# New words for the order of pieces in the two mixers, the two cross attentions and the two blocks

## The reference

```python
for layer in range(2):                       # first_block
    x = x + 0.5 * swiglu(rms_norm(x, ...), w_gate, w_up, w_down)
    h = rms_norm(x, mix_norm[layer])
    x = x + (diff_stickbreak_mixer if layer == 0 else mla_mixer)(h, ...)
    x = x + memory_cross_attention(rms_norm(x, ...), rms_norm(mem, ...), ...)
    x = x + 0.5 * swiglu(rms_norm(x, ...), ...)
for l in range(2):                           # second_block
    h = x @ w_cols
    mix = concat(gla(h_gla), rwkv7(h_rwkv), nsa(h_nsa)) @ w_out[l]
    x = layer_norm(ALPHA * x + mix, ...)
    x = layer_norm(ALPHA * x + swiglu(x, ...), ...)
```

## Time and profile before

| | us |
|---|---|
| median of 3 runs | 2518.86 (2516.48 to 2523.28) |
| the profiled execution | 2525.97 |
| its span, first to last instruction | 2524.2 |
| mean granted TensorE clock | 0.887 |
| PE, DVE, ACT, POOL busy | 2163.8, 1607.8, 1127.3, 433.6 |
| m0, from 208.1 to 426.0 | 217.9 |
| c0, from 426.0 to 497.0 | 71.0 |
| m1, from 876.0 to 1082.0 | 206.0 |
| c1, from 1082.0 to 1145.5 | 63.5 |
| b0, from 1336.3 to 1717.5 | 381.2 |
| b1, from 1919.9 to 2317.0 | 397.1 |

### The profile page before, as it was taken

The page is one execution under the profiler, slowest core; times in us unless marked ns, Lnnn a source line. Parts: engine busy times, 40 slices in busy tenths (PEclk is TensorE's granted clock), DMA queues, the critical chain, the costliest instruction groups (busy, mean ns, idle before and its releaser), DMA issues.

```text
span 2524.2 us, 33226 instructions
## 1 busy us (share of the span) xinstructions
PE 2163.8 (86%) x12512; PEld 1870.8 (74%) x12512; DVE 1607.8 (64%) x2915; ACT 1127.3 (45%) x2001; POOL 433.6 (17%) x393
## 2 busy tenths in 40 slices
PE   6999867699999977779999767879998766978997
PEld 6888756588888866767889555777887654767886
DVE  6867654487687667557765763646765674455765
ACT  4645562365465444335544412326544521234553
POOL 2410011122122100013200210001221120000223
PEclk9999887799999988789999876878998887678998
DMA  6555322155555532125554212014553212102552
GB/s 240 186 183 166 117 67 74 60 180 182 190 184 177 184 117 79 48 73 186 189 179 140 86 43 95 1 60 163 185 174 107 103 57 69 43 1 92 190 178 91
DMA packets 88720, 311.59 MB, mean 123 GB/s; under 512 B 9840, under 2 KB 12144, under 8 KB 88048
## 3 DMA queue, kind: packets, MB, share of 16 engines
q1 hardware_dynamic: 88272, 305.55, 37.1%
q10 hardware_dynamic: 288, 3.92, 0.4%
HBM read 308.38 MB, written 1.05 MB: 123 GB/s over the span
## 4 chain that ended last, share of the span: by engine, by line
PE 77%; DVE 14%; ACT 5%; issue 3%; POOL 1%; DMA 1%; DVEq 0%; SPq 0%; ACTq 0%; POOLq 0%
PE ps L124 74%; DVE scratch L139 5%; PE ps L129 3%; DVE w_lo L139 2%; ACT w_hi L134 2%; ACT scratch L134 1%; DVE stats L156 1%; DVE scratch L166 1%; DVE stats L151 1%; DVE scratch L145 1%; ACT scratch L165 1%; DVE stats L139 1%; DMA ring<-in_w 1%; ACT h L134 0%; POOL rows L139 0%
## 5 line engine op out<-in xcount | busy, mean ns | idle before, releaser
L139 DVE TENSOR_TENSOR w_lo<-ring,w_hi 128x1024 fp32r<-128x1024 f32 (+2 forms) x571 | 692.1, 1226 | 440.2 <-ACT w_hi L134 429.3
L124 PE MATMUL ps<-h,w_hi 128*128 128x512 f32 (+1 forms) x2720 | 877.4, 380 | 46.0 <-DVE h L151 19.1
L134 ACT ACTIVATE w_hi<-ring 128x1024 fp32r<-128x1024 f32 (+2 forms) x571 | 582.2, 1033 | 507.2 <-PE ps L124 500.2
L124 PE MATMUL ps<-h,w_lo 128*128 128x256 f32 x2416 | 687.1, 284 | 0.0
L124 PEld LDWEIGHTS ps<-h,w_hi 128*128 128x128 f32 x2720 | 503.6, 194 | 150.3 <-issue 32.1
L124 PEld LDWEIGHTS ps<-h,w_lo 128*128 128x128 f32 x2416 | 466.5, 193 | 0.0
L124 PE MATMUL ps<-f,w_hi 128*128 128x512 f32 (+1 forms) x1444 | 425.3, 360 | 6.0 <-DVE f L139 6.0
L124 PE MATMUL ps<-scratch 64*128 64x128 f32 (+10 forms) x2016 | 331.5, 358 | 72.7 <-DVE scratch L139 27.8
L124 PEld LDWEIGHTS ps<-scratch 64*128 64x128 f32 (+4 forms) x2016 | 280.6, 236 | 119.7 <-issue 51.2
L124 PE MATMUL ps<-f,w_lo 128*128 128x256 f32 x1184 | 334.9, 283 | 0.0
L124 PEld LDWEIGHTS ps<-f,w_hi 128*128 128x128 f32 x1444 | 259.4, 193 | 49.6 <-DVE w_lo L139 5.1
(11 more groups left out here) (122 smaller groups left out, 2152.7 us busy)
## 6 DMA issues: line engine op xcount, KB each, us to landing
ring<-in_w SPq DMA_DIRECT2D x520, 512.0 KB, 3.6
ring<-in_w SPq DMA_DIRECT2D x48, 384.0 KB, 3.8
ring<-in_w SPq DMA_DIRECT2D x16, 396.0 KB, 4.3
stage_consts<-in_cthree ACTq DMA_DIRECT2D x1, 1916.0 KB, 8.5
stage_consts<-in_ctwo ACTq DMA_DIRECT2D x1, 1915.0 KB, 7.5
stage_consts<-in_cone SPq DMA_DIRECT2D x1, 1339.0 KB, 6.5
ring<-in_w SPq DMA_DIRECT2D x9, 128.0 KB, 3.8
x<-in_x SPq DMA_DIRECT2D x4, 256.0 KB, 4.6
```

The lines of the kernel that those rows point to most:

```text
L124: return self.e.matmul(out, lhsT, rhs, start=start, stop=stop, skip_group_check=free)
L134: return self.e.activation(out, x, func, **k)
L139: return self.e.tensor_tensor(out, a, b, op)
```

## The change

Six words of the table WEAVE are replaced by others with the same letters, each as often as before. No function changes. What moves, told by pieces:

- m0: rs0 stands before lqa0; nk and both halves of qb come before lva; lva and ck0 come behind the first stick's first step; ck1 and ck2 stand together behind the third stick's first step; the first steps of sticks 7 and 6 come before sub0 and ck5, which stand together; the last steps of both come behind the first two turns of the output.
- m1: rs0 first; ck1 and ck2 before uq0; ck3 and ck4 behind hk; ck5 between kT5 and kT6; ck6 and ck7 late among the attention steps, whose lanes go in a regular round.
- c0, c1: another order of the lanes.
- b0: rp0 to rp4 without gp0 between them; rw2 before ga; rkk, rbon and rdec further ahead and np0 behind rdec; the delta rule from ri6 on before more of nc1 and of the attention.
- b1: ga before gp1; np0 before rkk; ri3 and ri4 before nk; ru, rG, rP and rS before or among nc1 and nS; the second round, from rm1,0 on, 13 places further ahead, with more attention steps behind its start.

```diff
--- before.py
+++ after.py
@@ -38,14 +38,14 @@
 
 
 WEAVE = {
-    "b0": ("rrgrrrrhgghhhghhhhhhrrrrhlhrrhhlrhhlrhhrrhrrhrhrrnrrnnnnnrnnrnwrnrnrnunnurwnrnuvurrwuruvuwrvrwru"
-           "ruvurrrrurvvrvrrwvrwrvrvrwrwvrwrvurwrwuwrrwuwrrrrvrrururvuvummmmmmmmmmmmmmmmmmmmmmmmmmmmmmmmmmmm"),
-    "b1": ("rrrrrrgrghghhhghhhrhhrhrhlhrrhhlhrrhlhrhrhrrrhrhnrrrnnrnnnnnrnrnrrnrnrunwvnurrnrvnruwurwrvuruwrv"
-           "urrvrrvruwrwrwvururvwrvrvwrvurwvruwrwurrrurrurwurvruwrwruvrvmmmmmmmmmmmmmmmmmmmmmmmmmmmmmmmmmmmm"),
-    "c0": ("ppppppcbdcbacbadadooooooooooooo"),
-    "c1": ("ppppppabdabcdabcdcooooooooooooo"),
-    "m0": ("qpqpqkykqbkvvkakbqbacsbbsaatbataasslsctacacssycaccyyactytcscattsscctostttstyyyooooooooooooooooo"),
-    "m1": ("yqpqqkqqkqqkqkqkkkhyttttttttuuuubcuayucuauyabacbbyababcabybacaabbcacbyaaybcabaccaacbccacbcoooooo"
+    "b0": ("rrrrrrgrhrgghrhhrhhhghhhrrhhhlrhhlhrhlhrrhrrhrrhnrrnnrrnnnnnrnrvnrwurwrnurnrnnrrnrnvrrurwvruwrru"
+           "rvrruwrrvuvrvrwruwvrururvwruwrvrurrrurvwruvrwuurwrvrwrwvvuwmmummmmmmmmmmmmmmmmmmmmmmmmmmmmmmmmmm"),
+    "b1": ("rrrrrrghggrhrhhlhrrhhghhhrhhrhhlhhrhlhrrhrrrrhrhnrrnrrnrrnnnnnrnrnrrnrrrnrurwnrvrnurrrrrnvrrnuru"
+           "vrwvruwrwrvuuvwrvuwrvurvwrurrrwrwrvruwrvuuwrvvruwwrvuurwvummwummmmmmmmmmmmmmmmmmmmmmmmmmmmmmmmmm"),
+    "c0": ("ppppppbadbacdbacdcooooooooooooo"),
+    "c1": ("ppppppbdabdcabdcacooooooooooooo"),
+    "m0": ("pqqqkkkpqbbkalbbaqsvyvstbkabactssyyacsaccastsctyaatccasttyctaccsttcacsoytsyyootsooooooooooooooo"),
+    "m1": ("pyqqqkkqyqyqqkqkqkkkhyyttttttyttuuuauuucuuabcaabccbabcaabccabbcaabccabbcyaabccabbcaayoaobcaboooo"
            "ooooooooooo"),
 }
 
```

## The result

The changed kernel takes 2443.8 us in the median of four runs (2442.4 to 2449.6), the kernel before beside it 2521.1: a ratio of 0.970, with a 95% interval of 0.968 to 0.972. Forecast were 2484 us and a range of 2450 to 2512. The sign was right and the size was not: 77 us went where 35 were forecast. The profiled execution has a span of 2440.4 us in place of 2524.2, 83.8 less.

The account below looks back on a forecast made before the run. TensorE and VectorE were taken to wait for each other in one fixed order, neither full; -7.5 (m0), -8.9 (m1), -1.8 (c0), -4.9 (b0) and -12.0 (b1) sum to -35.1 us, from 2518.9 to 2484, range 2450 to 2512.

Parts of the forecast that it names:

- the stop before rs0 with its cost: m0's start: TensorE idles 4.5 us before rs0 and a slow half projection adds 2.7, sum +7.2 us.
- The walks of VectorE in m0 and b1's front: VectorE's queue walked in new order with old durations: m0 -7.5, -6.7, -0.5 us; b1's front -6.5.
- b1's rm1,0: In b1, the second round's first product was to come about 26 us earlier.
- The work is the same piece by piece: All six stages: no matmul, split or transfer added or removed, so moves were costed with the trace's old times.
- a loss of 2.7 forecast: m0's start: half projection after the stop takes 8.30 us at clock 0.67 instead of 5.60, 2.7 more.
- -16.0: m1, first kT to output projection: 17.8 us of TensorE work gone, ck5's stop adds 1.8; between -20 and -12.
- +14.4: b1's last stretch: 20.3 us of work enters, 5.9 covered by idle time; ends +4.7 and +20.3.
- the slower rival: Blocks' mean clock falls from 0.78 to 0.737, cancelling the gain; at 0.72 the time is 2534 us; chance 0.07.
- a third of the idle time closes: m0, m1, b0, b1: 90 of 270 us idle may go, giving 2429 us; centre 2445, chance 0.12.
- No change: Seven or eight new look-ahead split stops in the two blocks eat 35 us; time 2518, chance 0.11.
- The clock rival: Blocks: waits among thinly spread small matmuls lower TensorE's granted clock, so the kernel gets slower; chance 0.07.
- theory B: From the experiments: TensorE's clock follows how much it stands still, so closing stops also speeds the matmuls around them.

Follow-up runs that it names:

- starts: Changed kernel with rs0 put back behind the first half projection in m0 and m1: 2442.1 us, ratio 0.968.
- m1_memory: Kernel before, with everything in m1 but the attention steps at its new places, the output's first two pieces still behind the attention: 2516.2 us, ratio 0.998.
- b1_held: Changed kernel with nS1, nS2 and eleven attention steps of b1 put back ahead of the second round: 2464.0 us, ratio 0.977.
- b1_dense: Kernel before, with every matmul of the attention steps of units 7 to 15 in b1 issued twice: 2533.7 us, ratio 1.004.
- m1_lanes: Kernel before, with only the 48 attention steps of m1 in the new regular round: 2523.7 us, ratio 1.001.
- m1_ck5: Changed kernel with the norm ck5 of m1 put back among the attention steps: 2450.4 us, ratio 0.973.

## Why the prediction was wrong in size and right in sign

The terms, in us, forecast and measured:

| place | forecast | measured |
|---|---|---|
| m0: start; to S0; to S5; to out; out | +7.2, -7.5, -6.7, -0.5, 0 | +7.0, -6.7, -9.7, -0.9, -1.9 |
| c0, c1 | -1.8, 0 | -5.0, +0.2 |
| m1: start; uq0; to kT0; to out; out | +0.7, +6.4, 0, -16.0, 0 | +1.3, +3.7, -1.0, -25.6, -3.1 |
| b0: front; to nc0; to rm1,0; to out; out | 0, -1.0, -6.6, +2.7, 0 | -0.7, -3.9, -5.2, +1.1, -2.8 |
| b1: front; to nc0; to rm1,0; to out; out | -6.5, +3.2, -23.1, +14.4, 0 | -5.8, +4.4, -27.4, +3.6, +2.3 |
| feed-forward stages | 0 | -7.7 |
| sum | -35.1 | -83.8 |

(The profiled execution of before lies 5 us above its median, that of after 1.5 us below, which is why the medians differ by 77 and the spans by 84.)

**What held.** The sign of every term that was not forecast at 0, and the stop before rs0 with its cost: 4.50 us and a slow lqa0 behind it, 7.0 in sum for 7.2, shown by putting rs0 back. That the price of the slow half projection fitted is in part luck: it was read behind m1's stop of 3.74 us, and behind that same stop the starts kernel lost nothing. The walks of VectorE in m0 and b1's front are within 1 us, except m0's middle, which was 3.0 us too small. uq0 came later, b1's rm1,0 came 28.8 us earlier (26 forecast), and its last stretch became longer. The sign rests on these.

**The step that failed: TensorE's clock was held fixed.** "The work is the same piece by piece", and so I moved pieces at the durations that they had. In this kernel a piece has no duration of its own. Of the 48.7 us between the two sums, 30.0 are matmuls that ran faster in the six stages (27.3 measured, against a loss of 2.7 forecast), 12.0 are idle time that closed beyond the forecast, and 6.7 lie in the feed-forward stages (by the stages' windows; the table ends f0 with TensorE's last instruction, 1 us earlier). The same steps of m1's attention took 50.0 us of TensorE (67.6 less 17.6) and then 41.6, at clocks of 0.80 and 0.94. Of the 9.6 us by which "-16.0" was too small, 8.4 are this, and the added matmuls show that the time is there to be had: they returned 6.9 us in the old order and 0.7 in the new. The same error stands in b1's "+14.4". I took 20.3 us in at the duration of the place that they left, where the clock is 0.66. An estimate from the windows: busy time by clock is 45.5 us of full-speed work before and 57.6 after, so 12.1 were added, 16.8 at the old clock of 0.72. The rise to 0.81 took 9.0 off that and closed idle time 4.2. (The estimate is good to some 2 us: for the same matmuls in m1_memory and in the changed kernel it gives 40.7 and 39.1.) That this stretch takes in work cheaply is shown by b1_held and, weaker, by b1_dense.

The Trainium skill (TensorE: Matmul & The Clock Gate, "A second HAM failure mode: psum-queue depth-cycling") says of one other kernel that small idle times between groups of matmuls came often enough to make the array swing between its two clocks. The trace agrees in part. In the last 41.7 us of m1's old attention the mean clock of 0.67 lies between the two levels, and the longest stops there are 3.32 and 2.89 us; but in the last 22.0 us of the new one TensorE also stops between groups, for 1.53 us and less, and the clock is 1.00. I had used this page for a loss at m0's start and for the slower rival. It works in both directions, and I did not ask what the clock would give back where an order closes stops.

**Rivals.** The first one, a third of the idle time closes (2445), gave the right number by luck: idle time in the six stages fell from 320.2 to 270.4 us, 16% and not a third, and the clock gave the rest. No change and slower are out. The clock rival named the right mechanism with the wrong sign.

**What the table credits wrongly to the change.** f4 and f5 are 2.3 and 3.3 us shorter in the new kernel. The forecast had them within 1 us. f5 is that much shorter in m1_memory too, where nothing near it changed, and 199.3 us in the second profile of the changed kernel, against 196.2 in the first and 198.9 before (from TensorE's first instruction to its last). And c0 with its old word took 71.0 or 68.7 us. So of the 83.8 us some 7 or 8 are this spread. The changed kernel's second set of runs, 2449.6 us at a ratio of 0.971, says the same: the gain is 72 to 77 us.

**What stays open.** Why the new order keeps the clock up, and why m1's two halves give +5.3 and -6.3 apart and the whole -25.6 (the two pieces of the output that neither half moves may have a part in it). By the earlier trace rows and the windows above, busy time is 8.4, 9.4 and 13.4 us above the changed kernel in the kernel before, in m1_lanes and in m1_memory, once the 17.6 us of memory halves are taken off the first two; m1_lanes also stands still 3.9 us longer. That books the difference but doesn't say when the clock falls, and theory B in its own words, how much TensorE stands still, is not enough: in kT0 to the output projection that is 12.3 us at a clock of 0.80 before and 12.7 at 0.94 after, in a shorter stretch. Nor does one long stop do it, since behind the 7.1 us of m1_ck5 the clock came back after 3.9 us. What is shown is that TensorE's matmuls ran faster at a higher granted clock in the new order, and that added work raises that clock in the old one. The idle time that closed in b0 and to nc0 beyond the walk (3.9 for 1.0) was not tested by itself.

## What to carry to other kernels

Before moving work between stretches, read the granted clock of both: convert a piece to full-speed work by the clock of the place that it leaves, and price it by the clock that the new place will have. No run here gives a rule for that clock, so let both of its levels stand as the ends of the range. Where a stretch has a low clock, work put there can be cheaper than its old duration says (b1's last stretch). Parts of an order may be worth little each and much together, so a part that fails alone is not yet refuted; and a long wait of TensorE on another engine can be filled with matmuls into the bank that it already owns, if they end before the wait does; that gave 1.7 us each in c0 and c1, nothing in m0, and no share of the whole time that the runs could show.

## What the runs showed of the hardware that was not expected

Added matmuls that compute nothing made all others of m1's old attention 6.9 us faster (clock 0.80 to 0.91) and those of the same matmuls in a better order only 0.7.

A stop of 3.74 us was followed by a clock of 0.67 in the kernel before and of 1.00 in starts, at the same place. Behind a stop of 7.1 us TensorE ran at 1.2 GHz for 3.9 us.

Stages with the same instructions in the same order differ by 2 to 4 us, between kernels and between two profiles of one kernel. In c0 (71.0 or 68.7 us with its old word) it is the clock, as shown above. In f5, whose order never changed, it is not. Its windows from TensorE's first instruction to its last, in m1_memory, in the changed kernel's first profile and in its second:

```profile
2307.00:2503.00 196.00, 190.83 (x1104) 168.65 (x1104) 129.29 (x203) 104.00 (x182) 50.73 (x43) 0.97 0.46 151
```

```profile
2236.50:2432.70 196.20, 191.04 (x1104) 168.87 (x1104) 128.93 (x203) 104.07 (x182) 51.56 (x43) 0.97 0.42 151
```

```profile
2236.90:2436.20 199.30, 194.14 (x1104) 169.25 (x1104) 128.83 (x203) 104.15 (x182) 51.46 (x43) 0.97 0.47 148
```

In the kernel before the same 1104 records took 198.9 us, 193.7 of them busy. The difference is spread over the stage at a clock of 1.00: where the stage is short, most windows of 20 us hold 117 or 118 records, where it is long, 115 or 116. The profiles say nothing of its cause. A gain of 3 us in one stage of one profile is therefore no evidence here.
